# Reordering the scatter of expert gates by token half, with one-hot gates for tokens 128 to 255 of expert tiles 0 to 87 only

## The chip, the cores and the metric

One NeuronCore of a Trainium2 chip runs the whole kernel. The metric is the device time of one execution in microseconds (us); lower is better. Matrix products run on TensorE (PE; its weight loads are PEld), element-wise work on VectorE (DVE) and ScalarE (ACT). GpSimd (POOL) and SyncE (SP) mostly issue DMAs.

## The reference

Two transformer blocks over 256 tokens of width 1024. The change touches the expert layer of the first block (PEER): 16384 experts, each a row of `expert_down` and a row of `expert_up`, of which every token picks 16 for each of 8 heads.

```python
cand = s1[..., :, None] + s2[..., None, :]          # top 16 x top 16 key pairs
top_s, top_pos = lax.top_k(cand, 16)
idx  = take_along_axis(i1 * 128 + i2, top_pos)      # the expert, per token, head and pick
gate = softmax(top_s)
act  = gelu(einsum("td,thkd->thk", xb, expert_down[idx]))
out  = einsum("thk,thkd->td", gate * act, expert_up[idx])
```

The kernel does this densely: it computes the gelu of every token with every expert, multiplies by a dense gate matrix that is zero where an expert was not picked, and multiplies with all rows of `expert_up`.

## The kernel before, in words

**Weight stream.** All weights pass as 412 tiles of 128 x 1024 f32 (512 KB). SP's queue loads two tiles at a time (1 MB) into one of the two halves of `raw`. ACT writes the rounded part `whi` (`split_hi`, L369), DVE the rest `wlo` (`split_lo`, L382) into a ring of 4 slots, three tiles ahead of PE (`LEAD`). PE does three products for each of eight 128-wide pieces: 24 matmuls of 256 columns per tile (`products`, L386 to L388). A load into a half of `raw` waits until both splits of the tiles in it are done.

**The expert layer** has two stages of 128 tiles. In the down stage (`hidden`, tiles `W_EXP` on) each tile gives 128 experts x 256 tokens; ACT writes their gelu to `ea[:, tile, :]` (`gelu`, L1119, L1123). In the up stage (tiles `W_UP` on; "up tile n" below) `ea[:, n, :]`, now gated, is split by ACT into `phi` (`p_hi`, L1130, L1135) and by DVE into `plo` (`p_lo`, L1595), and PE adds its product with the tile to the output (`add_outer`).

**Gates, first way: scatter.** DVE finds the picks head by head during the down stage (`candidates`, `choose`, `locate`, `weigh`; the last step, L1511, raises `pick`). POOL then issues 256 indirect DMAs (L343), each adding 128 gates (one per token of a half, one head, one pick) into the zeroed DRAM tensor `gates_dense`, which is laid out [tile][expert][token]. The order is head, token half `tb`, pick. Before each head POOL waits until all scatters of the earlier heads have landed. After all 256, POOL reads the gates of four tiles at a time into `gd` (two buffers, L351), and DVE multiplies them into `ea` (`apply`, L1591). This serves up tiles 56 to 127 (`SPLIT` = 56).

**Gates, second way: one-hot products.** For up tiles 0 to 55, PE transposes the picks (L792), and in the last 48 tiles of the down stage (`GROUPS_AT` = 80 on) DVE and PE make the gates in 64 groups of `GT` = 4 tokens, in steps of 2, 1 and 1 groups per tile (`GROUPS_OF`). A group is: one-hot of the second key (L1528), one-hot of the first key (L1529), that one-hot times three bf16 parts of the gate (L1535), twelve matmuls of 56 columns (`gate_group`, L799), and DVE's product from PSUM into `ea` (`apply_gates`, L1551).

**Order in the up stage.** In the step in which PE works up to tile n, DVE does, for n counted as in `output_step`: `apply(n + 2)`, `p_lo(n + 1)`, `split_lo` of tile n + 3. ACT does `p_hi(n)`, then `split_hi` of tile n + 3. Each engine runs its own list strictly in order.

Of the kernel before, what the change touches and what calls it, by code (L numbers as in the profile page):

```python
# [17 lines left out]
BF16 = mybir.dt.bfloat16  # L18
U32 = mybir.dt.uint32
ALU = mybir.AluOpType  # L20
# [3 lines left out]
P = 128  # L24
# [16 lines left out]
SPLIT = 56  # L41
GT = 4
N_GROUPS = T // GT
CHOSEN_AT = 76
GROUPS_AT = 80
GROUPS_OF = (2, 1, 1)
# [50 lines left out]
def program(nc, x_t, vecs, wts, c1, gate_w, rows, w_pool, keys, c2, ple_t, out):  # L97
    ctx = ExitStack()
    with ctx:
# [50 lines left out]
        kT = place("kT", [2, T], BF16, at=aux)  # L150
        gT = place("gT", [3, T], BF16, at=aux)
        grest = place("grest", [T], at=aux)
        iota = place("iota", [P, GT], BF16, at=aux)
        oh2 = place("oh2", [2, P, GT], BF16, at=aux)
        assert aux[0] <= small + 4 * KT * T
        aux = [aux_end]
        oh1 = place("oh1", [2, 3, SPLIT, GT], BF16, at=aux)
# [135 lines left out]
        def _(sp):  # L293
# [5 lines left out]
            with sp.Fori(1, N_TILES // 4) as i:  # L299
                for p in range(2):  # L300

                    sp.wait_ge(s["w_hi"], i * 4 + (2 * p - 2))
                    sp.wait_ge(s["w_lo"], i * 4 + (2 * p - 2))
                    sp.dma_start(raw[:, p, :], wts[bass.ds(i * 2 + p, 1), :, :].rearrange("a p n -> p (a n)"))\
                      .then_inc(rs[p], 16)
# [7 lines left out]
        def _(pl):  # L313
# [32 lines left out]
            pl.wait_ge(s["scat"], 16 * TB * TOPK * NH)  # L346
            by_tile = dense.rearrange("(n p t) o -> p n (t o)", p=P, t=T)
            for quad in range(SPLIT // 4, N_EXP // 4):
                n = quad - SPLIT // 4
                pl.wait_ge(s["g_mul"], N_GROUPS + (4 * (n - 1) if n >= 2 else 0))  # L350
                pl.dma_start(gd[:, n % 2, :, :], by_tile[:, 4 * quad:4 * quad + 4, :])\  # L351
                  .then_inc((s["gd0"], s["gd1"])[n % 2], 16)
# [208 lines left out]
        def _(pe):  # L561
# [220 lines left out]
            for n in range(CHOSEN_AT, GROUPS_AT):  # L782
# [3 lines left out]
                if n == CHOSEN_AT:  # L786

                    pe.wait_ge(s["pick"], NH)
                    for q in range(3):
                        for tb in range(TB):  # L790
                            picks = (key[:, 0, tb], key[:, 1, tb], gate[:, tb])[q].rearrange("p h k -> p (h k)")
                            m = nc.tensor.transpose(bank(2, P, base=q * T + tb * P), picks, ident[:, :])  # L792
# [12 lines left out]
            def gated_steps(i, first=False):  # L805
                g = 0
                for n in range(12):
                    for _ in range(GROUPS_OF[n % 3]):
                        pe.wait_ge(s["oh1"], i * 16 + (g + 1))
                        if not first or g >= 2:  # L810
                            pe.wait_ge(s["g_mul"], i * 16 + (g - 1))
                        gate_group(g % 2)
                        g += 1
                    pe.wait_ge(s["w_lo"], i * 12 + (W_EXP + GROUPS_AT + n + 1))
                    pe.wait_ge(s["gelu"], i * 12 + (GROUPS_AT + n - 1))
                    hidden(n % 4, n % 2)

            gated_steps(0, True)
            with pe.Fori(1, (N_EXP - GROUPS_AT) // 12) as i:
                gated_steps(i)  # L820

# [173 lines left out]
        def _(act):  # L995
# [129 lines left out]
            def p_hi(n, quad=None, gated=0):  # L1125
                if quad is None:
                    act.wait_ge(s["g_mul"], N_GROUPS)
# [3 lines left out]
                else:  # L1131
                    if gated:
                        act.wait_ge(s["g_mul"], quad * 4 + (N_GROUPS - SPLIT + n + 1))
# [758 lines left out]
```

## Time and profile before

| | |
|---|---|
| Time, median of 3 runs | 1472.79 us (1471.66 to 1476.47) |
| Profiled execution, its own time | 1471.94 us |
| Its span, first to last instruction | 1470.1 us |
| PE busy | 1369.1 us (93%) |
| DVE busy | 1005.5 us (68%) |
| ACT busy | 710.8 us (48%) |
| POOL busy | 512.2 us (35%) |
| Mean granted TensorE clock | 0.973 of full speed |

All times inside the kernel are counted from the start of the span. The profile lists matmuls as pipelined, so a busy PE is not PE at its peak; where PE stands still, the timeline shows idle time before the next matmul. The granted clock is given as a share of 2.4 GHz. The down stage of the expert layer runs from about 247 to 666 us, the up stage from 667 to about 1067 us.

### The profile page before, as it was taken

The page shows a single profiled execution, that of the slowest core. Times are in us where ns is not written, and L with a number is a line of the kernel's source. Part 1 is how long each engine was busy: PE and PEld are TensorE (multiplying, and loading weights), DVE is VectorE, ACT ScalarE, POOL GpSimd, SP SyncE. Part 2 cuts the span into 40 slices and gives each one's busy share as a digit, 9 for nine tenths or more (in the row PEclk, how much of TensorE's full clock was granted, in tenths as well). Part 3 has the DMA queues.
Part 4 walks back from the last instruction along what each step waited for, and adds up shares of the span by engine and source line. Part 5 has one row for each costly group of instructions (what it writes and reads, how often), then busy time and mean ns, then how long its engine had stood idle before and what let it go on. Part 6 is the DMA issues. An engine that isn't in the chain of part 4 may idle for free.

```text
span 1470.1 us, 30627 instructions
## 1 busy us (share of the span) xinstructions
PE 1369.1 (93%) x11396; PEld 1339.1 (91%) x11396; DVE 1005.5 (68%) x1904; ACT 710.8 (48%) x1034; POOL 512.2 (35%) x292
## 2 busy tenths in 40 slices
PE   6989999999999999999999469999998998999986
PEld 5889899999999999999999469999978897999986
DVE  6766577988997777775555246666686657666665
ACT  5832456777776333334444224444454444444443
POOL 1000001888687878787987810000000000000000
PEclk9999999999999999999999779999999998999998
DMA  7960344666666555556666456666654333555532
GB/s 252 384 270 2 144 135 153 172 172 178 193 172 177 144 140 144 120 138 171 175 188 180 86 161 225 230 226 217 224 178 144 115 115 125 192 174 195 177 115 86
DMA packets 74935, 249.50 MB, mean 170 GB/s; under 512 B 40768, under 2 KB 40896, under 8 KB 48112
## 3 DMA queue, kind: packets, MB, share of 16 engines
q1 hardware_dynamic: 30528, 218.22, 42.3%
q0 software_dynamic: 44336, 30.33, 11.4%
q8 instruction: 45, 0.74, 0.2%
q14 instruction: 26, 0.21, 0.0%
HBM read 230.57 MB, written 17.96 MB: 169 GB/s over the span
## 4 chain that ended last, share of the span: by engine, by line
PE 44%; POOL 32%; issue 8%; DVE 8%; DMA 5%; ACT 3%; SPq 0%; DVEq 0%; ACTq 0%; POOLq 0%
POOL gates_dense L343 32%; PE ps L386 13%; PE ps L387 13%; PE ps L388 13%; DMA gates_dense<-gate,spot 3%; DMA raw<-in_wts 3%; DVE wlo L382 2%; ACT whi L369 1%; DVE h L529 1%; DVE sq L466 1%; DVE alo L550 1%; PE ps L494 1%; PE ps L742 1%; PE ps L661 0%; PE ps L650 0%
## 5 line engine op out<-in xcount | busy, mean ns | idle before, releaser
L382 DVE TENSOR_TENSOR wlo<-raw,whi 128x1024 fp32r<-128x1024 f32 x412 | 502.8, 1222 | 169.5 <-ACT whi L369 157.4
L369 ACT ACTIVATE whi<-raw 128x1024 fp32r<-128x1024 f32 x412 | 435.0, 1058 | 351.0 <-PE ps L388 305.6
L386 PE MATMUL ps<-ahi,whi 128*128 128x256 f32 x2016 | 584.7, 290 | 19.4 <-DVE alo L550 9.2
L387 PE MATMUL ps<-alo,whi 128*128 128x256 f32 x2016 | 573.7, 285 | 0.0
L388 PE MATMUL ps<-ahi,wlo 128*128 128x256 f32 x2016 | 573.1, 284 | 0.0
L343 POOL DMA_INDIRECT gates_dense<-gate,spot x256 | 487.8, 1906 | 172.5 <-issue 87.5
L386 PEld LDWEIGHTS ps<-ahi,whi 128*128 128x128 f32 x2016 | 390.7, 194 | 28.0 <-issue 15.8
L387 PEld LDWEIGHTS ps<-alo,whi 128*128 128x128 f32 x2016 | 390.2, 194 | 0.2 <-issue 0.2
L388 PEld LDWEIGHTS ps<-ahi,wlo 128*128 128x128 f32 x2016 | 389.8, 193 | 0.0
L386 PE MATMUL ps<-phi,whi 128*128 128x256 f32 x1200 | 338.0, 282 | 32.4 <-DVE plo L1595 32.3
L387 PE MATMUL ps<-plo,whi 128*128 128x256 f32 x1200 | 340.8, 284 | 0.0
L388 PE MATMUL ps<-phi,wlo 128*128 128x256 f32 x1200 | 340.2, 283 | 0.0
L386 PEld LDWEIGHTS ps<-phi,whi 128*128 128x128 f32 x1200 | 229.6, 191 | 33.0 <-DVE plo L1595 32.8
L388 PEld LDWEIGHTS ps<-phi,wlo 128*128 128x128 f32 x1200 | 226.5, 189 | 0.0
L387 PEld LDWEIGHTS ps<-plo,whi 128*128 128x128 f32 x1200 | 225.9, 188 | 0.0
L1595 DVE TENSOR_TENSOR plo<-ea,phi 128x256 fp32r<-128x256 f32 x128 | 54.5, 426 | 145.8 <-ACT phi L1135 140.1
L1123 ACT ACTIVATE ea<-ps 128x256 f32 (+1 forms) x120 | 46.2, 385 | 156.9 <-PE ps L388 156.7
L351 POOL DMA_DIRECT2D gd<-gates_dense x18 | 13.7, 759 | 176.2 <-DVE ea L1591 174.5
L1135 ACT ACTIVATE phi<-ea 128x256 fp32r x124 | 49.5, 399 | 30.1 <-DVE ea L1591 30.1
L799 PE MATMUL ps<-oh,oh 128*128 128x56 bf16 x768 | 52.6, 234 | 2.0 <-DVE ea L1551 1.3
L1591 DVE TENSOR_TENSOR ea<-ea,gd 128x256 f32 (+1 forms) x72 | 30.1, 418 | 33.3 <-DMA gd<-gates_dense 33.3
L799 PEld LDWEIGHTS ps<-oh,oh 128*128 128x128 bf16 x768 | 42.9, 118 | 6.2 <-issue 3.3
(331 smaller groups left out, 1045.7 us busy)
## 6 DMA issues: line engine op xcount, KB each, us to landing
raw<-in_wts SPq DMA_DIRECT2D x206, 1024.0 KB
gates_dense<-pf POOLq DMA_DIRECT2D x4, 4096.0 KB, 16.9
gd<-gates_dense POOLq DMA_DIRECT2D x18, 512.0 KB, 5.9
gates_dense<-gate,spot POOLq DMA_INDIRECT x256
cst<-in_c POOLq DMA_DIRECT2D x1, 1216.0 KB, 12.6
x<-in_x_t SPq DMA_DIRECT2D x1, 1024.0 KB, 5.0
kk<-in_keys POOLq DMA_DIRECT2D x1, 1024.0 KB, 5.0
out_dram<-h SPq DMA_DIRECT2D x4, 256.0 KB, 2.5
```

Source lines behind the costliest of these rows:

```text
L343: pl.indirect_dma_start(out=dense, out_offset=bass.IndirectOffsetOnAxis(ap=spot[:, tb, h, k:k + 1], axis=0), in_=gate[:, tb, h, k:k + 1], ...
L369: nc.scalar.activation(whi[:, j, :], raw_tile(j // 2, j % 2), ACT.Copy).then_inc(s["w_hi"], 1)
L382: nc.vector.tensor_tensor(wlo[:, j, :], raw_tile(j // 2, j % 2), whi[:, j, :].bitcast(F32), ALU.subtract).then_inc(s["w_lo"], 1)
L386: nc.tensor.matmul(out_ap, wh, xh, start=first, stop=False, skip_group_check=True)
L387: nc.tensor.matmul(out_ap, wh, xl, start=False, stop=False, skip_group_check=True)
L388: return nc.tensor.matmul(out_ap, wl, xh, start=False, stop=last, skip_group_check=True)
L466: ch(nc.vector.tensor_tensor(pair(sq, 0), pair(sq, 0), pair(sq, q), ALU.add))
L799: m = tm(bank(2 + j, SPLIT, base=t * SPLIT), oh2[:, j, :, t], oh1[:, j, part, :, t], start=part == 0, stop=part == 2)
L1123: A(row_of(quad * 4 + n), bank(n % 2, T), ACT.Gelu).then_inc(s["gelu"], 1)
L1135: A(phi[:, n % 2, :], row_of(quad * 4 + n), ACT.Copy).then_inc(s["p_hi"], 1)
L1591: V.tensor_tensor(row_of(e), row_of(e), gd[:, n // 4 % 2, n % 4, :], ALU.mult).then_inc(s["g_mul"], 1)
L1595: V.tensor_tensor(plo[:, n % 2, :], row_of(oct_ * 8 + n), phi[:, n % 2, :].bitcast(F32), ALU.subtract)\
```

## The change

- The scatter's loops are exchanged: token half outermost, then head, then pick. A wait for all earlier scatters stands before each of the 16 (half, head) batches instead of before each head.
- `SPLIT` goes from 56 to 88, and the one-hot way serves only tokens 128 to 255 of up tiles 0 to 87: 32 groups instead of 64, one per tile, in down tiles 92 to 123 (`GROUPS_AT` = 92, `CHOSEN_AT` = 88). The operands grow from 56 to 88 first keys: L1529 works on 352 elements instead of 224, L1535 on 1056 instead of 672, `apply_gates` on 352 instead of 224, and the twelve matmuls have 88 columns. Three of the six transposes go.
- All other gates are read from `gates_dense`: tokens 0 to 127 of up tiles 0 to 87 (128 wide, once the first half of the scatter has landed), and all 256 tokens of up tiles 88 to 127 (once all of it has landed). SP's queue issues these reads, each before the weights of the same four tiles; POOL issues none.
- DVE's `apply` now runs for all 128 up tiles, 128 wide for the first 88; `p_hi` waits for it in each.
- Between the two stages DVE does two `apply`, three `split_lo` and `p_lo(0)` before it waits for the last gelu, which `p_lo(0)` came after before.
- Some tiles of SBUF change places (`oh1`, `oh2`, `kT`, `gT`, `grest`).

```diff
-SPLIT = 56
+SPLIT = 88
-N_GROUPS = T // GT
-CHOSEN_AT = 76
-GROUPS_AT = 80
-GROUPS_OF = (2, 1, 1)
+N_GROUPS = P // GT
+CHOSEN_AT = 88
+GROUPS_AT = 92
...
+            with sp.Fori(1, W_UP // 4) as i:
+                weights(i)
+            weights(W_UP // 4)
+            sp.wait_ge(s["scat"], 16 * TOPK * NH)
+            sp.wait_ge(s["g_mul"], N_GROUPS)
+            for par in range(2):
+                gates_of(0, par, P)
+            weights(W_UP // 4 + 1)
+            def up_pair(j, width):
+                for par in range(2):
+                    sp.wait_ge(s["g_mul"], j * 8 + (N_GROUPS + 4 * par - 4))
+                    gates_of(j, par, width)
+                    weights(j * 2 + (W_UP // 4 + par))
+            with sp.Fori(1, SPLIT // 8) as j:
+                up_pair(j, P)
+            sp.wait_ge(s["scat"], 16 * TB * TOPK * NH)
+            with sp.Fori(SPLIT // 8, N_EXP // 8) as j:
+                up_pair(j, T)
...
-            for h in range(NH):
-                pl.wait_ge(s["pick"], h + 1)
-                if h:
-                    pl.wait_ge(s["scat"], 16 * TB * TOPK * h)
-                for tb in range(TB):
+            for tb in range(TB):
+                for h in range(NH):
+                    pl.wait_ge(s["pick"], h + 1)
+                    if tb or h:
+                        pl.wait_ge(s["scat"], 16 * TOPK * (tb * NH + h))
                     for k in range(TOPK):
                         pl.indirect_dma_start(...)
...
+            dve.wait_ge(s["gelu"], 2)
+            lo_for(W_UP - 4)
+            apply(0, 0, P)
+            lo_for(W_UP - 3)
+            apply(1, 0, P)
+            lo_for(W_UP - 2)
+            p_lo(0, 0)
+            lo_for(W_UP - 1)
             dve.wait_ge(s["gelu"], N_EXP)
-            p_lo(0, 0)
```

`gates_of(j, par, width)` reads `gates_dense` for tiles 8j + 4par to 8j + 4par + 3, the first `width` tokens, into `gd[:, par]`; `weights(i)` is the old body of SP's loop (two loads of 1 MB, with their waits). `lo_for(u)` is `split_lo` of tile u + 3.

## Rows read from the trace of the kernel before

**Rows 1.** Stretches: length, busy time and count by engine, granted clock, DMA share, GB/s

```profile
681.00:820.00 139.00, 139.00 (x1160) 139.00 (x1160) 75.75 (x97) 65.66 (x97) 118.64 (x48) 1.00 0.63 181
829.00:851.00 22.00, 0.00 (x0) 0.00 (x0) 0.00 (x0) 0.00 (x0) 17.76 (x12) 0.50 0.23 0
875.00:1055.00 180.00, 180.00 (x1503) 180.00 (x1502) 118.28 (x188) 85.33 (x126) 11.27 (x15) 1.00 0.63 226
```

**Rows 2.** Timeline, 849 to 862 us: start, duration, instruction, idle before it

```profile
851.80 1.63 POOL L351 DMA_DIRECT2D gd<-gates_dense  x2 [1.69 <-DMA gates_dense<-gate,spot]
856.12 0.42 DVE L1591 TENSOR_TENSOR ea<-ea,gd 128x256 f32<-128x256 f32 x1 [33.30 <-DMA gd<-gates_dense]
...
856.94 0.58 PE L386 MATMUL ps<-phi,whi 128*128 128x256 f32 x1 [31.35 <-DVE plo L1595]
```

**Rows 3.** Timeline of DVE in the up stage

```profile
815.50 0.43 DVE L1595 TENSOR_TENSOR plo<-ea,phi 128x256 fp32r<-128x256 f32 x1 [1.32 <-ACT phi L1135]
...
872.85 0.43 DVE L1595 TENSOR_TENSOR plo<-ea,phi 128x256 fp32r<-128x256 f32 x1 [0.98 <-ACT phi L1135]
...
884.37 0.43 DVE L1595 TENSOR_TENSOR plo<-ea,phi 128x256 fp32r<-128x256 f32 x1 [0.98 <-ACT phi L1135]
...
887.37 0.43 DVE L1595 TENSOR_TENSOR plo<-ea,phi 128x256 fp32r<-128x256 f32 x1 [1.10 <-ACT phi L1135]
```

**Rows 4.** Timeline of ACT, gelus of down tiles 79, 126 and 127

```profile
478.09 0.39 ACT L1119 ACTIVATE ea<-ps 128x256 f32<-128x256 f32 x1 [1.54 <-PE ps L388]
...
662.39 0.39 ACT L1119 ACTIVATE ea<-ps 128x256 f32<-128x256 f32 x1 [2.26 <-PE ps L388]
...
665.98 0.38 ACT L1160 ACTIVATE ea<-ps 128x256 f32<-128x256 f32 x1 [0.26 <-PE ps L388]
```

**Rows 5.** Groups by form, 482 to 664 us: busy us, mean ns, idle before

```profile
L799 PE MATMUL ps<-oh,oh 128*128 128x56 bf16 x744 | 51.1, 234 | 2.0 <-DVE ea L1551 1.3
...
L1535 DVE TENSOR_TENSOR oh<-oheq,gT 128x672 bf16<-128x672 bf16 x61 | 31.0, 509 | 6.2
L1528 DVE TENSOR_TENSOR oh<-iota,kT 128x512 bf16<-128x512 bf16 x61 | 25.6, 420 | 0.0
L1551 DVE TENSOR_TENSOR ea<-ea,ps 128x224 f32 x48 | 18.3, 380 | 0.0
L1529 DVE TENSOR_TENSOR oheq<-iota,kT 128x224 bf16<-128x224 bf16 x61 | 16.5, 270 | 0.0
```

**Rows 6.** Timeline of PE, first matmul of the up stage

```profile
666.93 0.39 PE L386 MATMUL ps<-phi,whi 128*128 128x256 f32 x1 [0.99 <-DVE plo L1595]
```

**Rows 7.** Timeline of POOL, first scatters of heads 0, 3, 6 and 7

```profile
249.62 1.83 POOL L343 DMA_INDIRECT gates_dense<-gate,spot  x1 [59.88 <-DVE gate L1511]
...
474.56 2.35 POOL L343 DMA_INDIRECT gates_dense<-gate,spot  x1 [4.64 <-DMA gates_dense<-gate,spot]
...
682.08 1.54 POOL L343 DMA_INDIRECT gates_dense<-gate,spot  x1 [4.55 <-DMA gates_dense<-gate,spot]
...
774.74 1.54 POOL L343 DMA_INDIRECT gates_dense<-gate,spot  x1 [2.23 <-DMA gates_dense<-gate,spot]
```

**Rows 8.** The scatters' line, 469 to 640 us: count, min/median/max ns, starts

```profile
L343 POOL DMA_INDIRECT gates_dense<-gate,spot x79: 1542/1602/2582, 467.4 to 638.1; - x79
```

**Rows 9.** The line of the last step of a head's picks

```profile
L1511 DVE TENSOR_TENSOR gate<-cv,gsum x8: 191/192/228, 248.6 to 459.7; 128x32 f32<-128x32 f32 x8
```

**Rows 10.** Waits, whole span: total us, times, longest

```profile
POOL gates_dense L343 <- DMA gates_dense<-gate,spot: 25.1, 7, 4.6
```

**Rows 11.** Timeline, 780 to 790 us, DVE

```profile
787.16 1.22 DVE L382 TENSOR_TENSOR wlo<-raw,whi 128x1024 fp32r<-128x1024 f32 x1
```

**Rows 12.** Timeline, 780 to 790 us, POOL

```profile
787.23 2.57 POOL L343 DMA_INDIRECT gates_dense<-gate,spot  x1 [0.30 <-issue]
```

**Rows 13.** DMA issues of the page: KB each, us to landing

```profile
x<-in_x_t SPq DMA_DIRECT2D x1, 1024.0 KB, 5.0
```

More of the change, by code:

```diff
@@ L298, in _, with weights @@
                 sp.dma_start(raw[:, p, :], wts[p]).then_inc(rs[p], 16)
-            with sp.Fori(1, N_TILES // 4) as i:
+            def weights(i):
                 for p in range(2):
@@ L805, in gated_steps @@
             def gated_steps(i, first=False):
[L806 to L816, printed above, removed]
+                for n in range(4):
+                    pe.wait_ge(s["oh1"], i * 4 + (n + 1))
+                    if not first or n >= 2:
+                        pe.wait_ge(s["g_mul"], i * 4 + (n - 1))
+                    gate_group(n % 2)
+                    pe.wait_ge(s["w_lo"], i * 4 + (W_EXP + GROUPS_AT + n + 1))
+                    pe.wait_ge(s["gelu"], i * 4 + (GROUPS_AT + n - 1))
+                    hidden(n, n % 2)
             gated_steps(0, True)
-            with pe.Fori(1, (N_EXP - GROUPS_AT) // 12) as i:
+            with pe.Fori(1, N_GROUPS // 4) as i:
                 gated_steps(i)
+            for n in range(GROUPS_AT + N_GROUPS, N_EXP):
+                pe.wait_ge(s["w_lo"], W_EXP + n + 1)
+                pe.wait_ge(s["gelu"], n - 1)
+                hidden(n % 4, n % 2)
             def add_outer(j, xh, xl):
@@ L1164, in _ @@
                 split_hi(act, W_UP + n + LEAD, (W_UP + n + LEAD) % 4)
-            for first, last, gated in ((4, SPLIT, 0), (SPLIT, N_EXP, 1)):
-                with act.Fori(first // 4, last // 4) as i:
-                    for n in range(4):
-                        p_hi(n, i, gated)
-                        split_hi(act, None, (W_UP + n + LEAD) % 4, i + (W_UP + n + LEAD) // 4)
+            with act.Fori(1, N_EXP // 4) as i:
+                for n in range(4):
+                    p_hi(n, i)
+                    split_hi(act, None, (W_UP + n + LEAD) % 4, i + (W_UP + n + LEAD) // 4)
             act.wait_ge(s["p_split"], N_EXP)
@@ L1554, in _ @@
             dve.wait_ge(s["idxT_sb"], 1)
[L1555 removed]
+            ch(V.tensor_tensor(grest[:, :], bank(2, P, base=2 * P), gT[:, 0, :], ALU.subtract))
             ch(V.tensor_copy(gT[:, 1, :], grest[:, :]))
@@ L1568, in hidden_steps @@
                 base = W_EXP + GROUPS_AT + LEAD
-                g = 0
-                for n in range(12):
-                    split_lo(dve, None, (base + n) % 4, i * 3 + (base + n) // 4)
-                    for _ in range(GROUPS_OF[n % 3]):
-                        if not last or g + 2 < 16:
-                            lay_out(g + 2, i)
-                        apply_gates(g, i)
-                        g += 1
-            rounds = (N_EXP - GROUPS_AT) // 12
-            with dve.Fori(0, rounds - 1) as i:
+                for n in range(4):
+                    split_lo(dve, None, (base + n) % 4, i + (base + n) // 4)
+                    if not last or n < 2:
+                        lay_out(n + 2, i)
+                    apply_gates(n, i)
+            dve.wait_ge(s["gelu"], SPLIT)
+            with dve.Fori(0, N_GROUPS // 4 - 1) as i:
                 hidden_steps(i)
-            hidden_steps(rounds - 1, True)
+            hidden_steps(N_GROUPS // 4 - 1, True)
+            assert W_EXP + GROUPS_AT + N_GROUPS == W_UP - 4
             row_of = lambda e: ea[:, e, :] if isinstance(e, int) else \
@@ L1596, in p_lo, with output_step @@
                  .then_inc(s["p_split"], 1)
-            def output_step(n, oct_, first, last):
-                if n + 2 >= first:
-                    apply(n + 2, oct_)
-                if n + 1 < last:
+            def output_step(n, oct_, first, last=False):
+                if not last or n < 6:
+                    apply(n + 2, oct_, T if n + 2 >= first else P)
+                if not last or n < 7:
                     p_lo(n + 1, oct_)
```

73 lines of the change are left out of this document (34 added, 39 removed).

## Prediction

> **What bounds the kernel now.** I read the stretches first. In the up stage PE is busy throughout both with one-hot gates (681 to 820 us: 1160 matmuls in 139 us) and with gates read from DRAM (875 to 1055 us: 1503 in 180 us) [rows 1]. Both are 24 x 0.12 = 2.88 us a tile: PE is the bound, and a gate multiplication on DVE costs PE nothing. Between the two PE, DVE and ACT do nothing while POOL alone is busy [rows 1]. The timeline names that hole: the first read of `gd` leaves at 851.80, held by the landing of the last scatter, its gates reach DVE at 856.12, and PE restarts at 856.94 after 31.35 us of idling [rows 2]. Its whole price shows in the rhythm of `plo`: from tile 52 (815.50) to tile 60 (872.85) 57.35 us pass where eight tiles should take 23.04 [rows 3]. That is 34.3 us, 31.35 of standing and 3.0 of matmuls at a granted clock that stood at 0.50 in the hole, the 1.2 GHz level [rows 1].
>
> The second place is the down stage: from the gelu of tile 79 to that of tile 127, 48 tiles take 187.9 us [rows 4], not 48 x 2.88 = 138.2; 64 groups of one-hot products are in PE's stream.
>
> So the change can give at two places, and what decides the first is when the last scatter lands.
>
> **The down stage.** A tile with one group takes 665.98 - 662.39 = 3.59, say 3.60 us [rows 4], so a group costs PE 0.72 us. After the change 32 tiles have one group and 16 have none: 32 x 3.60 + 16 x 2.88 = 161.3 us. **Gain 26.6 us**, more than 32 x 0.72 = 23.0, because the steps with two groups cost extra (49.7 us for 64 groups are 0.78 each). The matmuls go from 56 to 88 columns. From 60 ns for 56 columns (0.72 / 12) to 120 ns for 256 the line rises 0.3 ns a column: at most 384 x 10 ns = 3.7 us of loss; nothing, if the weight loads set these 60 ns. I take nothing and keep 3.7. DVE in such a tile: `wlo` 1.22 [rows 11], plus 0.42, 0.27, 0.51 and 0.38 [rows 5], the last three scaled by 88/56 to 0.42, 0.80 and 0.60: 3.46 of 3.60 us even if none overlap, and its lead is one tile. Hidden, narrowly. Without that cover it is 0.1 us a tile. The three transposes that go are below 1 us; left out.
>
> The up stage then starts at 666.93 - 26.6 = 640.3 [rows 6], if the new start is no dearer. There SP issues the first gates only after the weight load that waits for the split of tile `W_UP` - 1, and DVE stands in `apply(0)` until they land: 5.0 us for 1 MB [rows 13] and a few for the gates. PE then still has most of four tiles of about 2.9 us in hand. Today's start has 0.99 us of idling [rows 6]; I count the two as equal, bounds -1 and +4.
>
> **The up stage.** The new `apply`, 128 wide, joins `plo` and `wlo`; with 256 wide ones DVE was busy 118.28 of 180 us [rows 1], and PE kept its pace. DMA: the scatter stretch has a share of 0.63 at 181 GB/s, the one with `gd` 0.63 at 226; adding the 45 GB/s of the latter to the former gives about 0.76. The gates of tiles m are issued some 7 tiles ahead behind one weight load, are needed 2 tiles ahead, and the next weights leave 5.8 us later. Cost nothing; if the 512-byte rows made a read of four tiles slow enough to push weights back, a few tenths per four tiles.
>
> **When does the last scatter land?** Count scatters.
> - *To 469 us* nothing changes but the order and twice the waits. Picks come every 30 us (248.6 to 459.7 for 8 [rows 9]), a batch of 16 takes longer, so POOL never waits for them. Before, 96 scatters took 474.56 - 249.62 = 224.9 us [rows 7]; a wait costs 25.1/7 = 3.6 us instead of 0.3, so 3.3 [rows 10]; less three waits, 2.24 us a scatter. A batch is 16 x 2.24 + 3.3 = 39.1 us; in 219.4 us: 90 scatters.
> - *469 to 640 us.* Before 79 starts in 171 us [rows 8], 2.04 each without three waits; with five waits 76. But in tiles 77 to 91 DVE has only `wlo`, which pins the scatters to one per tile (next point): 15 instead of 21. So 70; total 160.
> - *Up stage.* Here the scatters take 2.57 us, not 1.54. One started at 787.23 while `wlo` ran from 787.16 to 788.38, and ended 1.42 us after `wlo` did [rows 11, 12]. It is held until DVE's instruction is over. Next start is 0.30 later, when the next `plo` and `wlo` already run: one scatter per tile. 32 of them took 774.74 - 682.08 = 92.7 us, 2.90 each, one wait included [rows 7]. The Trainium skill (SBUF — State Buffer, "Who interferes with whom") says that a DVE instruction with two SBUF inputs contends with GpSimd's reads, yet infers that `tensor_tensor` leaves descriptor generation alone; by the latter scatters would keep 1.84 us and my rival A would follow. The row above speaks against the latter. 86 tiles of 2.88 us give 85 scatters. In the stage with `apply`, though, one `plo` in eight comes 0.12 us late (884.37 to 887.37 is 3.00 [rows 3]); a scatter could slip in before `wlo` there, at most 11 more. I take 5: total 250 when PE has done up tile 85, at 640.3 + 86 x 2.88 = 888.0.
> - SP waits for all 256 before the gates of tile 88, and behind that wait stand the weights of tile 88. ACT needs them for `split_hi(88)`, in front of `p_hi(86)`. So the hole now opens before tile 86, at 888.0. Then DVE idles and scatters come every 1.84 us (1.54 + 0.30): 6 x 1.84 + 3 for landing: **902 us**.
>
> To lift the hole, SP's queue brings 512 KB of gates and then 1 MB of weights: 5.0 [rows 13] + 1.8 for the gates (512 KB at 181/0.63 = 287 GB/s [rows 1]) + `whi`, `phi`, `plo` 1.9 = 8.5 us with the issue hidden in it. Hole 902 + 8.5 - 888 = 22.5, with the clock 3.0: 25.5 us against 34.3. **Gain 8.8 us.**
>
> **Sum.** 1470.1 - 26.6 - 8.8 = 1434.7 us of span. The execution's own time is 1.8 above its span and the median 0.9 above that: 1437.4. I predict **1437 us**.
>
> **Rivals.**
> - *A: the hole closes.* If the last scatter lands by about 880 us, before SP needs it, both gains are full: 1470.1 - 26.6 - 34.3 + 2.7 = 1412. It takes some 10 scatters above my count by then, as with all 11 slips and no pinning in tiles 77 to 91 (+12). For it: `apply` perturbs a rhythm of DVE and POOL that is exact to hundredths; against: in 681 to 820 us the pinning never let go by itself but after a wait. The skill's inference would give it too (640 + 96 x 1.84 + waits is 833 us). Chance 0.22, down to 1424 with a small hole.
> - *B: the hole is longer, but not by what was gained.* With 83 scatters in the up stage and 67 instead of 70 before it, 240 are out at 888; 16 x 1.84, one more wait (3.3) and 3 for landing end near 924: hole 47.5 us with the clock, 1459. Chance 0.10 for 1452 to 1468.
> - *C: slower than before.* The new `apply` is a third instruction with two SBUF inputs in each up tile. If the hold passes on to it and the scatter misses its turn every second tile, 43 scatters pass in 248 us; 53 are left, which at 1.84 and with three waits land at 996: hole 120 us, 1532. It decides once fewer than about 232 are out by 888, a pace above 3.4 us. Against: with four such instructions a tile the down stage has 2.04 [rows 8]. Chance 0.06.
> - *The change does only half:* no gain at the hole, the down stage alone: 1446. It lies inside my own range.
>
> **Chances.** My case, 1424 to 1452: 0.60; A 0.22; B 0.10; within 0.3% (4.4 us, about what a measurement here can tell from no change) 0.02; C 0.06. Range to 8 in 10: 1411 to 1456. Faster 0.92, same 0.02, slower 0.06.
>
> **What would show it.** Down tiles with a group at 3.6 us; 32 groups of L799 with 384 matmuls; the up stage starting near 640; scatters of 2.57 us in it at one per tile, some 160 out before it; one PE hole of about 22 us before up tile 86, with a granted clock at 0.50, ended by a weight load behind the gates. Wrong if: PE has no hole (A), scatters take above 3.4 us (C), ACT waits for `raw` every four tiles, or PE idles for more than 4 us at the start of the up stage.

## The result: 1422.68 us, and the profile after

The changed kernel takes **1422.68 us** (median of four runs, 1419.46 to 1425.53), the kernel before on the same chip 1472.69 (1471.66 to 1476.47): a ratio of 0.9655, interval [0.9627, 0.9684]. The profiled execution took 1424.04 with a span of 1422.2. That lies in the range, 14 us below the forecast and just outside my own case (1424 to 1452): the hole that was predicted to stay at 25.5 us is gone, as in rival A, and the down stage gave 16.5 us instead of 26.6.

The page of the changed kernel: busy time of the engines, the chain that ended last, three groups (busy us, mean ns, idle before).

```profile
PE 1352.4 (95%) x11009; PEld 1325.3 (93%) x11009; DVE 981.9 (69%) x1832; ACT 718.3 (51%) x1040; POOL 505.2 (36%) x274
...
PE 82%; DVE 7%; ACT 4%; DMA 3%; issue 3%; ACTq 0%; SPq 0%; DVEq 0%
...
L413 PE MATMUL ps<-phi,whi 128*128 128x256 f32 x1200 | 339.4, 283 | 2.0 <-DVE plo L1618 2.0
...
L1614 DVE TENSOR_TENSOR ea<-ea,gd 128x128 f32 (+3 forms) x128 | 41.8, 326 | 6.6 <-DMA gd<-gates_dense 6.6
...
L825 PE MATMUL ps<-oh,oh 128*128 128x88 bf16 x384 | 37.4, 263 | 0.0
```

In the first up-stage group PE now idles 2.0 us for `plo` in all, where one wait of 31.35 stood before [rows 2]. DVE's one wait for `gd` is 6.6 us, at the start of the up stage. 384 matmuls of 88 columns are the 32 groups of the prediction.

**The down stage.** Three gelus of tiles with one group, and the gelu of tile 127 (timeline of ACT, changed kernel):

```profile
595.59 0.39 ACT L1150 ACTIVATE ea<-ps 128x256 f32 x1 [2.44 <-PE ps L415]
...
599.50 0.39 ACT L1150 ACTIVATE ea<-ps 128x256 f32 x1 [2.58 <-PE ps L415]
...
603.41 0.39 ACT L1150 ACTIVATE ea<-ps 128x256 f32 x1 [2.58 <-PE ps L415]
...
650.02 0.38 ACT L1186 ACTIVATE ea<-ps 128x256 f32<-128x256 f32 x1 [1.04 <-PE ps L415]
```

A tile with a group takes 3.91 us (599.50 to 603.41), not 3.60 [rows 4]. The stage, from the gelu of tile 79 at 478.6, lasts 171.4 us against 187.9: a gain of 16.5. ACT waits for PE in each of them, and PE has no wait between 530 and 620 us, so it is PE that is slower: a group costs it 3.91 - 2.88 = 1.03 us, 86 ns for each of 12 matmuls, with the change from one kind of matmul to the other in it.

**The start of the up stage** (timelines of DVE and PE, changed kernel):

```profile
648.24 0.29 DVE L1614 TENSOR_TENSOR ea<-ea,gd 128x128 f32<-128x128 f32 x1 [6.63 <-DMA gd<-gates_dense]
...
650.92 0.42 DVE L1618 TENSOR_TENSOR plo<-ea,phi 128x256 fp32r<-128x256 f32 x1
```

```profile
651.40 0.38 PE L413 MATMUL ps<-phi,whi 128*128 128x256 f32 x1 [1.41 <-DVE plo L1618]
```

DVE does stand in `apply(0)`, for 6.63 us, and PE idles 1.41 us where it idled 0.99 [rows 6]. The stretch in front of the up stage hides the new reads, as counted.

**The up stage.** Stretches (length, busy time and instructions of PE, PEld, DVE, ACT, POOL, granted clock, DMA share, GB/s):

```profile
660.00:820.00 160.00, 160.00 (x1336) 160.00 (x1335) 97.99 (x167) 75.55 (x111) 127.48 (x60) 1.00 0.70 202
829.00:851.00 22.00, 22.00 (x186) 22.00 (x185) 13.57 (x23) 10.14 (x16) 14.95 (x8) 1.00 0.70 215
```

The second row is the stretch in which all but POOL stood at a granted clock of 0.50 before [rows 1]. Now PE is busy in all of it, at 1.00, the 2.4 GHz level; POOL still scatters beside it. From the first `plo` (650.92) to the last (1016.81) the stage takes 365.89 us; before it was 399.36. Gain 33.5, nearly the whole price of the hole. With 15.5 from a start that comes earlier (666.45 against 650.92) and 1.1 lost behind the stage the span is accounted for: 15.5 + 33.5 - 1.1 = 47.9 = 1470.1 - 1422.2.

**Where the hole was expected**, before up tile 86: the last scatter and SP's queue (timelines of POOL and SP, changed kernel).

```profile
878.98 2.58 POOL L377 DMA_INDIRECT gates_dense<-gate,spot  x1 [0.30 <-issue]
```

```profile
875.19 0.38 SPq L314 DMA_DIRECT2D gd<-gates_dense  x1
880.36 6.09 SPq L306 DMA_DIRECT2D raw<-in_wts  x2
886.96 0.38 SPq L314 DMA_DIRECT2D gd<-gates_dense  x1
891.88 6.09 SPq L306 DMA_DIRECT2D raw<-in_wts  x2
898.28 0.38 SPq L314 DMA_DIRECT2D gd<-gates_dense  x1
```

The last scatter ends at 881.56. SP issues gates at 875.19, 886.96 and 898.28: the second, those of tile 88 and behind the wait for all scatters, falls in the regular beat (11.8 and 11.3 us). SP did not have to wait for the scatters there; how near it was is worked out from run e2 below.

**Why the scatters were done.** The scatters' line in two stretches (count; min/median/max ns; first and last start), and POOL's waits for landings (total us, times, longest), changed kernel:

```profile
L377 POOL DMA_INDIRECT gates_dense<-gate,spot x75: 1541/1552/2592, 468.5 to 639.0; - x75
...
L377 POOL DMA_INDIRECT gates_dense<-gate,spot x60: 1541/2575/2594, 657.9 to 819.3; - x60
```

```profile
POOL gates_dense L377 <- DMA gates_dense<-gate,spot: 46.6, 14, 4.9
```

Started by 469 us: 93 (counted 90). From 469 to 512, tiles 77 to 91: 17 (counted 15). To 640: 57 (counted 55). So each of these three stretches gave two or three more than its count, and a surplus of seven stood before the up stage. The 89 that were left took 241 us, to 881.56; by the prediction's pace (90 in 247.7 us) they take 245. Their landing is seen some 1.7 us later (e2 below), near 883.3, where the prediction had 902. Of these 19 us, 14 are the surplus (with it the prediction's own pace brings the landing to 888), and the other 5 are the pace and a landing of 1.7 instead of 3 us. Most scatters of the up stage are of 2.57 us, held by `wlo` as [rows 11, 12] show. One in sixteen tiles slips (timelines of DVE and POOL, changed kernel):

```profile
720.17 0.43 DVE L1618 TENSOR_TENSOR plo<-ea,phi 128x256 fp32r<-128x256 f32 x1 [1.12 <-ACT phi L1161]
...
723.17 0.43 DVE L1618 TENSOR_TENSOR plo<-ea,phi 128x256 fp32r<-128x256 f32 x1 [1.24 <-ACT phi L1161]
723.52 1.22 DVE L409 TENSOR_TENSOR wlo<-raw,whi 128x1024 fp32r<-128x1024 f32 x1
```

```profile
720.58 2.58 POOL L377 DMA_INDIRECT gates_dense<-gate,spot  x1 [0.30 <-issue]
723.46 1.56 POOL L377 DMA_INDIRECT gates_dense<-gate,spot  x1 [0.30 <-issue]
725.32 1.54 POOL L377 DMA_INDIRECT gates_dense<-gate,spot  x1 [0.30 <-issue]
727.17 1.75 POOL L377 DMA_INDIRECT gates_dense<-gate,spot  x1 [0.31 <-issue]
```

`plo` is 0.12 us late (3.00 us after the one before), so `wlo` comes at 723.52, just behind the scatter's start at 723.46, and that scatter and two more pass unheld.

### The profile page after: what moved, and what is told of

Its sections match the earlier page's. It is cut to its first block, busy times and chain, and to the rows that moved or that the text cites. A ratio compares the mean times of both kernels' runs of the same rounds, so it can differ in the third digit from the quotient of the medians.

```text
span 1422.2 us, 29762 instructions
## 1 busy us (share of the span) xinstructions
PE 1352.4 (95%) x11009; PEld 1325.3 (93%) x11009; DVE 981.9 (69%) x1832; ACT 718.3 (51%) x1040; POOL 505.2 (36%) x274
## 4 chain that ended last, share of the span: by engine, by line
PE 82%; DVE 7%; ACT 4%; DMA 3%; issue 3%; ACTq 0%; SPq 0%; DVEq 0%
PE ps L413 25%; PE ps L414 25%; PE ps L415 25%; DMA raw<-in_wts 3%; PE ps L825 2%; DVE wlo L409 1%; ACT whi L396 1%; DVE h L556 1%; ACT L1150 1%; PE ps L521 1%; PE ps L769 1%; PE ps L688 1%; DVE alo L577 0%; PE ps L677 0%; ACT L396 0%
## 5 line engine op out<-in xcount | busy, mean ns | idle before, releaser
L377 POOL DMA_INDIRECT gates_dense<-gate,spot x256 | 494.5, 1932 | 196.9 <-issue 89.7
L413 PEld LDWEIGHTS ps<-ahi,whi 128*128 128x128 f32 x2016 | 390.4, 194 | 26.6 <-issue 16.8
L415 PE MATMUL ps<-phi,wlo 128*128 128x256 f32 x1200 | 336.8, 281 | 0.0
L413 PEld LDWEIGHTS ps<-phi,whi 128*128 128x128 f32 x1200 | 225.0, 187 | 2.6 <-DVE plo L1618 2.4
L1150 ACT ACTIVATE ea<-ps 128x256 f32 x120 | 46.1, 384 | 136.5 <-PE ps L415 121.5
L1614 DVE TENSOR_TENSOR ea<-ea,gd 128x128 f32 (+3 forms) x128 | 41.8, 326 | 6.6 <-DMA gd<-gates_dense 6.6
L825 PE MATMUL ps<-oh,oh 128*128 128x88 bf16 x384 | 37.4, 263 | 0.0
L825 PEld LDWEIGHTS ps<-oh,oh 128*128 128x128 bf16 x384 | 30.4, 118 | 1.4
```

The source lines that it names most:

```text
L377: pl.indirect_dma_start(out=dense, out_offset=bass.IndirectOffsetOnAxis(ap=spot[:, tb, h, k:k + 1], axis=0), in_=gate[:, tb, h, k:k + 1], ...
L413: nc.tensor.matmul(out_ap, wh, xh, start=first, stop=False, skip_group_check=True)
L415: return nc.tensor.matmul(out_ap, wl, xh, start=False, stop=last, skip_group_check=True)
L825: m = tm(bank(2 + j, SPLIT, base=t * SPLIT), oh2[:, j, :, t], oh1[:, j, part, :, t], start=part == 0, stop=part == 2)
L1150: A(row_of(quad * 4 + n), bank(n % 2, T), ACT.Gelu).then_inc(s["gelu"], 1)
L1614: V.tensor_tensor(v, v, gd[:, n // 4 % 2, n % 4, 0:width], ALU.mult).then_inc(s["g_mul"], 1)
```

## The experiments

Theory 1: the stepped read of `oh1` (88 elements, 8 bytes apart) sets what a group costs. Theory 2: the hole is a deadline: SP's wait for all scatters has to be met before PE reaches tile 86, and what the down stage gains on one side of it is lost on the other. Theory 3: the pace of the scatters is set by the 1.22 us of a single `wlo`. Rivals are named with each run.

**e1: 56 columns again** (the gates of keys 56 to 87 are left out).

```diff
-m = tm(bank(2 + j, SPLIT, base=t * SPLIT), oh2[:, j, :, t], oh1[:, j, part, :, t],
+m = tm(bank(2 + j, 56, base=t * SPLIT), oh2[:, j, :, t], oh1[:, j, part, 0:56, t],
```

> The changed kernel, with one edit: the twelve matmuls of a group read 56 of the 88 columns (the gates of first keys 56 to 87 are left out of the product, so the output is not the reference's). Theory 1 (a group costs PE two cycles of 2.4 GHz per column plus some 13 ns a matmul, 60 ns at 56 columns and 86 ns at 88): a tile with a group goes from 3.9 back to 3.60 us, and the up stage starts about 10 us earlier, near 641. Rival (the longer DVE instructions set the 3.9 us): no change, 3.9 us a tile. Theory 2 (the last scatter lands just in time for SP only because the down stage is long): scatters land near 888 as before or a little later, SP now needs them near 877, and a hole of 5 to 10 us opens on PE before up tile 86, so that the span is 1417 to 1422, not 1412. Rival: there is slack, no hole, 1412.

Measured: 1431.48 us in one run, span 1429.7. Timelines of ACT and PE, e1:

```profile
516.81 0.39 ACT L1150 ACTIVATE ea<-ps 128x256 f32 x1 [2.36 <-PE ps L415]
...
520.41 0.39 ACT L1150 ACTIVATE ea<-ps 128x256 f32 x1 [2.27 <-PE ps L415]
```

```profile
905.75 0.58 PE L413 MATMUL ps<-phi,whi 128*128 128x256 f32 x1 [16.31 <-DVE plo L1618]
```

A tile takes the predicted 3.60 us and the up stage starts at 641.0, where the prediction had 640.3. And the hole opens before tile 86: its `plo` is at 905.27, where 640.5 + 86 x 2.88 = 888.2 is due. The last scatter ends at 893.64. The prediction's stage times bring the prediction's hole, at 19.0 instead of 25.5 us (from `plo` 0 to `plo` 127: 384.84 against 365.89). The expectation had 5 to 10 us of hole and a span of 1417 to 1422, and missed. Ten microseconds less of down stage made the span of this one run 7.5 us longer, since the last scatter ended 12 us later than in the changed kernel. Its trace shows where: the twelfth batch of 16 starts at 668.0 instead of 662.7 us, and the four behind it take 185 us instead of 178. Of the 19.0 us, 16.3 are idling and the rest is a slow clock, granted 0.50 behind the hole (906 to 910 us), the 1.2 GHz level. Gates leave at 895.38, 1.7 us behind the last scatter, and PE restarts 10.4 us after that, where the prediction had 8.5.

**e2: 88 adjacent columns** (each matmul reads a run of 88 elements as it lies, so tokens 128 to 255 get other gates in tiles 0 to 87).

```diff
+flat1 = oh1[:, j, part, :, :].rearrange("p e t -> p (e t)")
-m = tm(..., oh2[:, j, :, t], oh1[:, j, part, :, t],
+m = tm(..., oh2[:, j, :, t], flat1[:, t * SPLIT:(t + 1) * SPLIT],
```

> The changed kernel, with one edit: the matmuls of a group read 88 adjacent columns of the same first-key operand instead of every fourth (so the gates are wrong and the output is not the reference's); DVE's work, the columns and the sizes stay. Theory 1a (what costs is the step of four elements between columns): 88 adjacent columns cost at most as much as 56 stepped ones, a tile with a group takes 3.60 us or less. Theory 1b (what costs is the number of columns, however they lie): 3.9 us as in the changed kernel. With 1a theory 2 expects again a hole of 5 to 10 us before up tile 86 and a time of 1417 to 1424; its rival 1412.

Measured: 1423.32 us (1422.96 to 1425.33), ratio to the kernel before 0.9668 [0.9652, 0.9684]. Timelines of SP and PE, e2:

```profile
889.22 0.38 SPq L314 DMA_DIRECT2D gd<-gates_dense  x1
889.96 0.91 SPq L306 DMA_DIRECT2D raw<-in_wts  x2
```

```profile
897.50 0.58 PE L413 MATMUL ps<-phi,whi 128*128 128x256 f32 x1 [14.19 <-DVE plo L1619]
```

A tile takes (621.84 - 515.37) / 31 = 3.434 us, 0.55 for the group, 46 ns a matmul, and PE has no wait in these tiles either: with the number of columns kept, the step alone takes a matmul from 46 to 86 ns. The up stage starts at 634.7, 16.7 us earlier than in the changed kernel, and the total is the same: the hole of 14.19 us of idling and its slow clock (382.84 - 365.89 = 17.0 us in the stage) took all of it. Gates are issued at 889.22, 1.7 us behind the end of the last scatter (887.49), and PE restarts 8.3 us later; the prediction had 8.5 for that chain. In the changed kernel the same 1.7 us behind 881.56 give 883.3, and SP comes by at 886.96: the margin was 3.7 us, one or two scatters. PE itself came to tile 86 at 899 us (651.40 + 86 x 2.88), so that with a chain of 8.3 (e2) to 10.4 us (e1) it would have stood only for a landing later than some 889 to 891 (an estimate).

**e3: `apply` on 8 tokens, not 128, in tiles 0 to 87** (the other 120 tokens go without a gate).

```diff
+width = 8 if width == P else width
 v = row_of(oct_ * 8 + n)[:, 0:width]
```

> The changed kernel, with one edit: for up tiles 0 to 87 the multiplication with the gates from DRAM works on 8 of the 128 tokens (the rest stay ungated, the output is not the reference's). It asks whether this third instruction changes the scatters' pace. If the slips (two scatters more per 16 up tiles, where one plo comes 0.12 us late) come from the waits and the loop of DVE and not from its length, the pace in the up stage stays 2.84 us and the span 1422. If its length matters, the pace goes to the 2.90 of the kernel before: two scatters fewer by 887 us, the last one lands some 5 us later, and a hole of 5 to 8 us appears: 1427 to 1431.

Measured: 1423.52 us in one run, span 1421.7. 89 scatters from 640 to 887 us, as in the changed kernel, the last ends at 880.61. The length of `apply` plays no part in the pace. What its mere presence does, this run leaves out. Rival C, which needed a pace above 3.4 us, is refuted by the result already: 89 scatters in 241 us are 2.7 each.

**e4: the kernel before with the scatters in the new order** (15 waits for landings, not 7; nothing else).

```diff
-for h in range(NH):
-    pl.wait_ge(s["pick"], h + 1)
-    if h: pl.wait_ge(s["scat"], 16 * TB * TOPK * h)
-    for tb in range(TB):
+for tb in range(TB):
+    for h in range(NH):
+        pl.wait_ge(s["pick"], h + 1)
+        if tb or h: pl.wait_ge(s["scat"], 16 * TOPK * (tb * NH + h))
```

> The kernel before, with only the scatter's loops exchanged (token half outermost, a wait before each of 16 batches). It prices the order alone: eight more waits. By the prediction's count (3.3 us a wait outside the up stage, about 0.5 where the scatters are pinned to one per tile; some five of the eight fall before 667 us) the last scatter lands 17 to 20 us later, PE's hole grows from 31.4 to about 50 and the time is 1488 to 1493. Rival (DVE's hold and the waits overlap, so that waits are nearly free): 1473 to 1478.

Measured: 1482.7 us (1480.21 to 1484.26), ratio 1.0062 [1.0045, 1.008]. Timeline of PE, e4:

```profile
869.07 0.58 PE L386 MATMUL ps<-phi,whi 128*128 128x256 f32 x1 [41.37 <-DVE plo L1595]
```

The time lies between the two expectations. The hole grows by the 10.0 us that PE idles more than [rows 2] say, and so does the time. The last scatter ends at 862.14, not 850.12: eight more waits cost 12 us, 1.5 each, not the 3.3 that I had given each outside the up stage. The list of waits shows the same size: POOL's waits for landings are 38.7 us in all (14 seen, 2.8 each) against 25.1 (7, 3.6 each) [rows 10]. Why each is shorter is open; a wait also moves the scatters behind it to a place ahead of `wlo`, where they pass in 1.54 us, but no run takes that apart. By itself the new order is a loss, and it is repaid by what it allows.

**e5: `p_lo` before `apply`** (the whole computation is kept).

```diff
-if not last or n < 6:
-    apply(n + 2, oct_, T if n + 2 >= first else P)
 if not last or n < 7:
     p_lo(n + 1, oct_)
+if not last or n < 6:
+    apply(n + 2, oct_, T if n + 2 >= first else P)
```

> The changed kernel, with one edit: in each step of the up stage DVE does p_lo(n + 1) before apply(n + 2) instead of after it, so that apply stands between plo and wlo. Theory 3 (a scatter is held while one DVE instruction with two SBUF inputs runs, and goes on at the end of that one instruction; the pinning comes from the request falling into wlo, right behind plo): the request now falls into apply, the scatter goes on 0.1 to 0.2 us later, and three scatters pass per two tiles: pace near 1.9 us instead of 2.84, the last one lands near 825 instead of 885. PE never waited for it in the changed kernel, so the time stays 1422 within 3 us. Rival (the scatter waits until DVE's whole run of instructions is over): pace stays 2.88 and more, the last scatter lands at 885 or later, a small hole may open.

Measured: 1420.69 us (1419.64 to 1422.93), ratio 0.9642 [0.9626, 0.9658], no more than the changed kernel can vary. The pace did not improve: 57 scatters run between 660 and 820 us, against 60. The expectation failed by its own sum: a `wlo` of 1.22 us in a rhythm of 2.88 begins 1.66 us behind the end of the last, and a held scatter that follows at 0.30 and needs 1.54 is not through by then, wherever `apply` stands. If that sum holds, what counts is the length of `wlo`, which the next run halves.

**e9: `split_lo` in two instructions in the up stage** (the whole computation is kept).

```diff
-split_lo(dve, None, u % 4, oct_ * 2 + u // 4)
+split_lo(dve, None, u % 4, oct_ * 2 + u // 4, halves=True)
 ...
+nc.vector.tensor_tensor(wlo[:, j, 0:h], raw_tile(...)[:, 0:h], whi[:, j, 0:h].bitcast(F32), ALU.subtract)
+nc.vector.tensor_tensor(wlo[:, j, h:TW], raw_tile(...)[:, h:TW], whi[:, j, h:TW].bitcast(F32), ALU.subtract)
```

> The changed kernel, with one edit: in the up stage split_lo writes wlo in two instructions of 512 columns instead of one of 1024. Theory 3, with its sum mended after e5_apply_late (whatever stands before it, a wlo of 1.22 us in a tile of 2.88 starts 1.66 us after the end of the last; a scatter let go there ends 1.42 later and the next asks 0.30 after that, at 1.72: 0.06 us too late): with halves of about 0.6 us the scatter is let go after the first half, three pass in two tiles, pace near 1.95 us instead of 2.84, the last lands near 835 instead of 885. PE did not wait for it, so the time stays at 1420 to 1425. Rival (the hold lasts for DVE's whole run of instructions): pace 2.88, landing at 885 or later.

Measured: 1420.77 us (1420.37 to 1423.66), ratio 0.9643 [0.962, 0.9665]. The scatters' line from 660 to 820 us, and timelines of DVE and POOL, e9:

```profile
L377 POOL DMA_INDIRECT gates_dense<-gate,spot x72: 1541/1542/1881, 659.9 to 819.4; - x72
```

```profile
718.65 0.43 DVE L1625 TENSOR_TENSOR plo<-ea,phi 128x256 fp32r<-128x256 f32 x1 [1.05 <-issue]
719.00 0.68 DVE L411 TENSOR_TENSOR wlo<-raw,whi 128x512 fp32r<-128x512 f32 x1
719.60 0.68 DVE L413 TENSOR_TENSOR wlo<-raw,whi 128x512 fp32r<-128x512 f32 x1
```

```profile
717.48 1.54 POOL L377 DMA_INDIRECT gates_dense<-gate,spot  x1 [0.30 <-issue]
719.33 1.76 POOL L377 DMA_INDIRECT gates_dense<-gate,spot  x1 [0.30 <-issue]
```

72 scatters instead of 60, none above 1.88 us, and the last ends at 836.90 instead of 881.56. The scatter of 719.33 meets the first half (to 719.68) and ends 1.41 us behind it, though the second half runs by then: it is held only to the end of the instruction that it meets, and so shorter instructions hold it less though DVE works longer (0.68 twice for 1.22). The time stays, as there was no hole left to close.

**e12: the kernel before with the same halves**, nothing else (the whole computation is kept).

```diff
-split_lo(dve, None, u % 4, oct_ * 2 + u // 4)
+split_lo(dve, None, u % 4, oct_ * 2 + u // 4, halves=True)
```

> The kernel before, with the edit of e9_wlo_halves alone. From 667 to 825 us its scatters were pinned at 2.9 us, 54 in 158 us. Theory 3: 80 in that time, so that all 256 have landed near 813, before PE reaches up tile 55 at 825; the hole of 31.4 us closes, and with it the 3 us of slow clock: 1472.6 - 34 = 1438 to 1442. Rival (the hold lasts for the whole run): 1472.

Measured: 1437.11 us (1436.5 to 1437.66), ratio 0.9746 [0.9726, 0.9767]. The scatters' line from 681 to 820 us, and PE's waits from 640 to 1100 us (total us, times, longest), e12:

```profile
L343 POOL DMA_INDIRECT gates_dense<-gate,spot x63: 1541/1542/2018, 679.7 to 808.6; - x63
```

```profile
PE ps L393 <- DVE plo L1602: 1.0, 1, 1.0
PE ps L883 <- DVE qk L1681: 0.5, 1, 0.5
PE ps L393 <- DVE wlo L389: 0.4, 1, 0.4
```

63 scatters pass in these 139 us, where 48 passed [rows 1], and the stretch even outlasts them: all are done at 810.12, 40 us earlier, and the hole is gone. The price that [rows 3] gave it, 34.3 us, is what one edit of `split_lo` brings: 1470.1 - 1435.6 = 34.5 us of span. The time is a microsecond below the expected 1438 to 1442. Neither e9 nor e12 has a hole, and they differ by 1437.11 - 1420.77 = 16.3 us: that is about the 16.5 of the down stage by itself. So of the 50 us between the two kernels, this one edit of the old kernel brings 35.

**e6, e7, e8: `oh1` laid out with the keys adjacent**, in e7 with `apply` behind `p_lo`, in e8 with the weights of tile 88 ahead of SP's wait (in e8 the gates of up tiles 88 to 95 are read from the place of those of tiles 0 to 7).

```diff
-oh1 = place("oh1", [2, 3, SPLIT, GT], BF16, at=aux)
+oh1 = place("oh1", [2, 3, GT, SPLIT], BF16, at=aux)
-m = tm(..., oh1[:, j, part, :, t],
+m = tm(..., oh1[:, j, part, t, :],
-V.tensor_tensor(oh1[:, j, :, :, :], ...
+V.tensor_tensor(oh1[:, j, :, :, :].rearrange("p q t e -> p q e t"), ...
```

> The changed kernel, with the first-key operand laid out with adjacent columns (oh1 as [part][token][key], DVE writing it in steps), so that the matmuls read what e2_contig_read read, with the right gates. Theory 1a: a tile with a group at 3.43 us as there, unless DVE's stepped write (L1560, 0.71 us before) grows by more than 0.4 us and DVE becomes the bound. By theory 2 nothing is gained all the same: a hole of about 14 us before up tile 86, span 1421 to 1424. Rival: 1408.

> Both edits, of e5_apply_late and e6_row_major. If theories 1a, 2 and 3 hold, the down stage ends some 15 us earlier and the scatters land 50 us before SP needs them: no hole, span 1422 - 15 = 1407, time 1405 to 1409. If theory 3 falls, 1421 to 1424.

> e6_row_major with, in SP's queue, the weights of up tiles 88 to 91 issued before the wait for all scatters instead of after the gates behind it. By the prediction's chain (the hole opens before tile 86 because the weights of tile 88 stand behind that wait) the hole now opens one tile later, before tile 87, and ends 2 to 3 us earlier after the last landing (no 1 MB and no whi in between): 14 us become 8 to 10, span 1415 to 1418. Rival (what matters is only the landing of the gates): as e6_row_major.

Measured: 1519.7 us (1518.13 to 1522.13), ratio 1.0317 [1.03, 1.0334]; 1520.89, 1.0324 [1.0307, 1.0341]; 1521.62, 1.033 [1.0312, 1.0347]. All three missed their times, and for one reason. Groups by form, 530 to 680 us, e6:

```profile
L1560 DVE TENSOR_TENSOR oh<-oheq,gT 128x1056 bf16<-128x1056 bf16 x22 | 106.2, 4825 | 2.7
...
L825 PE MATMUL ps<-oh,oh 128*128 128x88 bf16 x252 | 15.7, 224 | 48.0 <-DVE ea L1576 48.0
```

I had moved the step from TensorE's read to DVE's write. The expectation named the danger, a growth by more than 0.4 us, but its times counted nothing for it. 1056 bf16 elements with 176 bytes between neighbours take DVE 4.83 us; the same product with adjacent writes takes 0.71 in the changed kernel (its group, 530 to 620 us):

```profile
L1560 DVE TENSOR_TENSOR oh<-oheq,gT 128x1056 bf16<-128x1056 bf16 x23 | 16.3, 709 | 2.8
```

DVE became the bound of the down stage, at about 7 us a tile, and PE waits 48.0 us for it in this stretch. Neither e7's question (does the order help) nor e8's (may the weights pass the wait) got an answer: the up stage starts at 748.7 us in e6, so late that no hole is left in it. They stay open.

**e10: keys adjacent, and DVE's writes adjacent too** (beside `oh1` and its read as in e6, `oheq` too is kept in the order token, key, its comparison is turned round accordingly, and the gate is repeated along the key by a step of zero; the whole computation is kept).

```diff
-oheq = place("oheq", [2, SPLIT, GT], BF16, at=aux)
+oheq = place("oheq", [2, GT, SPLIT], BF16, at=aux)
-V.tensor_tensor(oh1[:, j, :, :, :], oheq[...].unsqueeze(1).to_broadcast([P, 3, SPLIT, GT]),
-                v.unsqueeze(2).to_broadcast([P, 3, SPLIT, GT]), ALU.mult)
+V.tensor_tensor(oh1[:, j, :, :, :], oheq[...].unsqueeze(1).to_broadcast([P, 3, GT, SPLIT]),
+                v.unsqueeze(3).to_broadcast([P, 3, GT, SPLIT]), ALU.mult)
```

> The changed kernel, with the first-key operand in rows of 88 adjacent keys as in e6_row_major, but DVE writes it in order and reads its inputs repeated along the key instead (the inner step of one input is 0), in place of the stepped write that took 4.8 us. If a repeated input runs at the rate of before (0.71 us for 1056 elements) PE sets the tile: 3.43 us, the up stage starts near 635 and, with the scatters as they are, a hole of some 14 us opens: 1421 to 1424. If it runs at one element a cycle (0.96 GHz, 1.1 us), DVE has about 3.5 us a tile and sets it: 3.5 to 3.6, with a hole of about 12 us and the same time. If it is as slow as the stepped write, 1520.

Measured: 1413.58 us (1412.89 to 1416.64), ratio 0.9595 [0.9572, 0.9617]. Groups by form, 530 to 640 us, e10:

```profile
L1561 DVE TENSOR_TENSOR oh<-oheq,gT 128x1056 bf16<-128x1056 bf16 x26 | 32.7, 1258 | 3.0
L826 PE MATMUL ps<-oh,oh 128*128 128x88 bf16 x312 | 16.7, 206 | 3.2 <-DVE ea L1577 1.7
```

The tile with a group takes 3.65 us, now by DVE, and the up stage starts at 641.0. The expectation had a hole of 12 us there and missed: the last scatter ended at 873.86, some 14 us before e2's, and PE has no hole. The traces show where these 14 us are. The twelfth batch of 16 starts at 656.5 us in e10 and at 662.3 in e2, and the four behind it take 177 us in e10 and 185 in e2: in e10 three unheld scatters come every 23 us (from 712.9, 735.9 and 759.0), in e2 every 46 (from 729.6, 775.7 and 821.8). Why they come more often in e10 no run settles. SP comes by at 876.39, less than a microsecond behind the landing.

**e13: e10 with the halves of e9 and `SPLIT` = 80**, one-hot gates for eight up tiles fewer, so that all scatters are needed eight tiles earlier (the whole computation is kept).

> The edits of e9_wlo_halves and e10_row_b together, and SPLIT = 80. In e10_row_b DVE set the 3.65 us of a tile with a group; with 80 first keys its three longer instructions lose 0.17 us together, so 3.48 to 3.55 us: the down stage ends 3 to 5 us earlier, near 636. SP needs all scatters eight tiles earlier than with SPLIT = 88, at about 636 + 73 x 2.88 = 846; with the halves they land near 840 as in e9_wlo_halves. No hole: 1408 to 1411. If one part of this fails (the halves' pace does not hold), a hole of 30 us and more opens before up tile 78, above 1440.

Measured: 1410.57 us (1409.75 to 1413.0), ratio 0.9586 [0.957, 0.9602]: 12 us below the changed kernel and the lowest of all, though its interval overlaps that of e10. Timeline of SP, e13:

```profile
838.48 0.38 SPq L315 DMA_DIRECT2D gd<-gates_dense  x1
843.64 6.10 SPq L307 DMA_DIRECT2D raw<-in_wts  x2
850.25 0.38 SPq L315 DMA_DIRECT2D gd<-gates_dense  x1
```

The last scatter ends at 847.12, the gates behind the wait leave at 850.25 in the beat of 11.8 us, and PE's one wait for a `plo` is 2.2 us at the start of the up stage. The landing came some 7 us later than expected, and with 1.7 us for it (e2) 1.4 us were left. A tile with a group takes (623.41 - 515.19) / 31 = 3.49 us. With the scatters faster the split can be earlier and a tile with a group cheaper, though by this margin hardly earlier than 80.

## Why the prediction was right and where it was wrong

- *The number:* the range held, but it held because rival A was in it, and the forecast of 1437 is as near as it is by luck. Two errors partly cancel: the hole at 25.5 us was none, and the down stage took 10 us more than its sum.
- *What bounds it, and where the change gives:* right. The hole and the down stage account for the result, and e12 confirms the price of the hole by itself (34.5 us against 34.3).
- *The down stage, "I take nothing and keep 3.7":* a failed step, and of the two the one whose bound was wrong as well. The loss was 10 us (e1 against the changed kernel: 641.0 and 651.4 at the start of the up stage). I had drawn the bound from a line between 56 columns in steps (60 ns) and 256 adjacent ones (120 ns), two kinds of read and two data types. From 60 ns at 56 to 86 at 88 stepped columns the slope is 0.81 ns a column; adjacent, 88 columns take 46 ns (e2), less than 56 stepped ones. The stepped read was in PE's time before too, and the one number of the trace did not show it.
- *DVE hidden in the tile, the start of the up stage equal, `apply` and the gates' reads at nothing:* right. The start cost 0.4 us more of PE's time, the up stage keeps 2.88 us a tile, and e3 takes nearly all of `apply` away for no gain. The DMA share was 0.70, where the prediction worked out 0.76.
- *The last scatter at 902:* too late by 19 us. The counts to 469, 512 and 640 us were low by three, two and two. A wait for a landing was put at its full 3.3 us; the eight more of e4 cost 1.5 each. In the up stage the slips came every 16 tiles, which is the 5 that were taken, and the pace was as counted within 2% (241 us for 89 against 245). A small slip in reading: of the 79 scatters in [rows 8] one started at 467.4 and belongs to the stretch before.
- *The chain behind the landing, 8.5 us:* its own terms add up to 8.7 (5.0 + 1.8 + 1.9). It measured 8.3 in e2 and 10.4 in e1.
- *"the hole now opens before tile 86, at 888.0":* this failed from both sides. 888.0 became some 899 as the down stage took 10 us longer and the start 0.4, and the scatters had landed at 883.3. e1 is the kernel of my own stage times, and it has the hole before tile 86. What the sum missed is that the two terms are coupled: near the deadline, time that the down stage loses is not added but taken from the hole. The coupling is not all of it: e1's last scatter also ended 12 us later than the changed kernel's, for a reason that no run shows. By itself neither would have closed the hole (estimates, with a chain of 8.3 to 10.4 us): with a landing as late as e1's (895.4) and PE at tile 86 at 899, 5 to 7 us are left, and with a landing at 883.3 and e1's PE at tile 86 at 889, 3 to 5 us. In e2 likewise 16.7 us were gained and 17.0 lost, but its last scatter ended 5.9 us later, so that the two are nearly equal by chance. The result was the time of rival A plus the 10 us: 1412 + 10 = 1422.
- *Rival A* named two reasons, slips in all of the late `plo` and no pinning in tiles 77 to 91. Neither came: slips were half as many, and pinning held (17 scatters in 43 us). It was the surplus of seven from before, and the later deadline. e1 had nearly the same surplus (166 scatters by 640 us against 167) and kept its hole, so the surplus alone did not close it.
- *The hold of scatters by `wlo`:* right, and now shown by change and not by reading alone: the same work in halves raises 48 scatters to 63 in 139 us (e12) and 60 to 72 in 160 (e9). The Trainium skill (SBUF — State Buffer, "Who interferes with whom") infers that `tensor_tensor` leaves descriptor generation alone; these indirect DMAs are held all the same, 2.57 us beside `wlo` and 1.54 without it. The same section of the Trainium skill has a `tensor_tensor` with both inputs in SBUF contend with GpSimd's reads, and a scatter reads its index tile `spot` in SBUF, so its hold may be that read; no run takes the two apart. By another rule of this section of the Trainium skill, that the blocked side waits until the instruction is over, e9 is as it should be.

## What to carry to other kernels

Where two engines meet at a deadline, work out the time of each side and take the later; gains ahead of it count only as far as the other side is early. In e1 (one run) a faster stage even lost, as the other side came later with it. A result that hangs on such a deadline is fragile: e2 and e10 differ by a few unheld scatters, and e2 has a hole of 14 us and e10 none. Price a matmul by the step of its operands, not by columns alone, and when a step is moved to another engine, price it there first. A queue that another engine's long instruction holds up can be freed by cutting that instruction, at a small cost to that engine (0.14 us a tile here): in e12 one edit was worth 35 us.

## What the runs showed of the hardware

- 88 moving bf16 columns at steps of 8 bytes: 86 ns a matmul (changed kernel); adjacent: 46 ns (e2). Both are the group's time divided by 12. The slope of 0.81 ns a stepped column is about two cycles of 2.4 GHz (worked out, from two points).
- DVE's product of 1056 bf16 elements: 0.71 us when the innermost step of all sides is one (changed kernel), 1.26 us when one input repeats an element along the innermost dimension, a step of zero (e10), 4.83 us when the output goes in steps of 176 bytes (e6). The Trainium skill (VectorE: DVE Perf Modes, "What auto-detection actually checks") says that the double rate needs every tensor 16 bits wide with a step of one. The first two agree with that, 1.26 being 1.8 times 0.71; that page of the Trainium skill gives no price for the third, which is 6.8 times the first.
- An indirect scatter that meets `wlo` (a `tensor_tensor` with both inputs in SBUF) is held to that instruction's end and then needs 1.42 us more [rows 11, 12]; cut in two, the instruction costs DVE 0.14 us more and the scatter 0.2 us instead of 1.03 (e9). Other DVE instructions were not tried.
